# The feed-forward part of a decoder block in panels of Strassen products, its output added up in memory

## The reference, cut to what matters

```python
h = h + merged @ w_out[l]
hn = rms_norm(h, norm_ffn_g[l])
h = h + (jax.nn.silu(hn @ w_ffn_gate[l]) * (hn @ w_ffn_up[l])) @ w_ffn_down[l]
```

## Time and profile before

| | us |
|---|---|
| median of 3 runs (1349.11 to 1349.36) | 1349.15 |
| span of the profiled execution | 1347.3 |
| PE busy, share of the span | 1331.1, 99% |
| DVE busy, share | 743.3, 55% |
| ACT busy, share | 606.4, 45% |
| POOL busy | 33.5, 2% |
| moved by DMA | 251.23 MB, 186 GB/s over the span |

### The profile page before, as it was taken

One profiled execution on the slowest core, in us unless ns is written; L12 is line 12 of the kernel. 1 busy time (PEld: TensorE's weight loads), 2 busy tenths in 40 slices (PEclk: granted clock), 3 DMA queues, 4 the chain that ended last, 5 costly groups with the idle time before them and its releaser, 6 DMA issues.

```text
span 1347.3 us, 16021 instructions
## 1 busy us (share of the span) xinstructions
PE 1331.1 (99%) x6224; PEld 1100.3 (82%) x6224; DVE 743.3 (55%) x938; ACT 606.4 (45%) x781; POOL 33.5 (2%) x34
## 2 busy tenths in 40 slices
PE   7999999999999999999999999999999999999998
PEld 6888887777788888888888888888888888888887
DVE  6556556777455555565555555455545554555553
ACT  5454545555444444444444443344444434444442
POOL 1112110000000000000000000000000000000000
PEclk9999999999999999999999999999999999999999
DMA  8655655444565555555565555555555556555552
GB/s 260 198 202 165 210 188 182 147 148 143 206 200 188 188 187 188 188 185 187 188 193 185 191 188 201 194 188 188 189 186 188 187 200 196 195 187 187 187 187 94
DMA packets 129943, 251.23 MB, mean 186 GB/s; under 512 B 4624, under 2 KB 10832, under 8 KB 129632
## 3 DMA queue, kind: packets, MB, share of 16 engines
q1 hardware_dynamic: 129600, 250.37, 56.5%
q0 software_dynamic: 288, 0.10, 0.1%
HBM read 248.33 MB, written 2.12 MB: 186 GB/s over the span
## 4 chain that ended last, share of the span: by engine, by line
PE 95%; ACT 3%; DVE 1%; issue 0%; DMA 0%; DVEq 0%; SPq 0%; ACTq 0%
PE bank L948 30%; PE bank L950 30%; PE bank L949 30%; PE bank L877 2%; ACT prob L594 1%; PE bank L892 1%; ACT w_hi L494 1%; PE bank L917 1%; DVE staged L657 0%; PE bank L919 0%; PE bank L902 0%; DMA x_rows<-in_x 0%; PE bank L918 0%; DVE xT_lo L665 0%; DVE w_lo L648 0%
## 5 line engine op out<-in xcount | busy, mean ns | idle before, releaser
L648 DVE TENSOR_TENSOR w_lo<-raw,w_hi 128x1024 fp32r<-128x1024 f32 (+1 forms) x464 | 562.5, 1216 | 556.1 <-ACT w_hi L494 554.2
L494 ACT ACTIVATE w_hi<-raw 128x1024 fp32r<-128x1024 f32 (+1 forms) x464 | 487.6, 1052 | 694.8 <-PE bank L950 693.2
L948 PE MATMUL bank<-w_hi,xT_hi 128*128 128x512 f32 (+1 forms) x1248 | 488.6, 391 | 4.2 <-DVE w_lo L648 3.0
L950 PE MATMUL bank<-w_lo,xT_hi 128*128 128x512 f32 (+1 forms) x1248 | 483.2, 387 | 0.0
L949 PE MATMUL bank<-w_hi,xT_lo 128*128 128x512 f32 (+1 forms) x1248 | 482.9, 387 | 0.0
L948 PEld LDWEIGHTS bank<-w_hi,xT_hi 128*128 128x128 f32 x1248 | 234.9, 188 | 53.7 <-issue 2.6
L950 PEld LDWEIGHTS bank<-w_lo,xT_hi 128*128 128x128 f32 x1248 | 234.9, 188 | 47.9
L949 PEld LDWEIGHTS bank<-w_hi,xT_lo 128*128 128x128 f32 x1248 | 235.1, 188 | 45.8
L948 PE MATMUL bank<-w_hi,oT_hi 128*128 128x512 f32 x480 | 187.0, 390 | 0.0
L950 PE MATMUL bank<-w_lo,oT_hi 128*128 128x512 f32 x480 | 186.8, 389 | 0.0
L949 PE MATMUL bank<-w_hi,oT_lo 128*128 128x512 f32 x480 | 186.7, 389 | 0.0
(11 more groups left out here) (109 smaller groups left out, 496.2 us busy)
## 6 DMA issues: line engine op xcount, KB each, us to landing
raw<-in_w_in SPq DMA_DIRECT2D x64, 1024.0 KB, 5.3
raw<-in_w_ffn_gate SPq DMA_DIRECT2D x44, 1024.0 KB, 5.2
raw<-in_w_ffn_up SPq DMA_DIRECT2D x44, 1024.0 KB, 5.1
raw<-in_w_ffn_down SPq DMA_DIRECT2D x44, 1024.0 KB, 5.0
raw<-in_w_out SPq DMA_DIRECT2D x16, 1024.0 KB, 5.0
raw<-in_w_branch_a SPq DMA_DIRECT2D x8, 1024.0 KB, 5.0
raw<-in_w_branch_b SPq DMA_DIRECT2D x8, 1024.0 KB, 4.9
x_rows<-in_x SPq DMA_DIRECT2D x4, 512.0 KB, 7.7
```

Source lines behind the costliest of these rows:

```text
L494: A(w_hi[:, p % SPLIT_SLOTS, 0:w], raw[:, c % RAW_SLOTS, (p % 2) * w:(p % 2 + 1) * w], ACT.Copy).then_inc(hi_ready, 1)
L648: V.tensor_tensor(w_lo[:, p % SPLIT_SLOTS, 0:w], raw[:, p // 2 % RAW_SLOTS, (p % 2) * w:(p % 2 + 1) * w], w_hi[:, p % SPLIT_SLOTS, 0:w].bi ...
L948: M(sums, x_hi, w_hi[:, p % SPLIT_SLOTS, w], start=kt == 0, stop=False)
L950: ins = M(sums, x_hi, w_lo[:, p % SPLIT_SLOTS, w], start=False, stop=kt == j.kts - 1)
```

## The change

The FFN leaves the list of jobs and gets 17 panels. A panel of kind `gu` takes one column of 512 of gate and the same of up, a panel `down` two output columns; so a panel has two weight columns and two token tiles. Its first eight k-tiles are seen as a 2 x 2 matrix of blocks: left operand [token tile][k half], weight [k half][column], a k half being four k-tiles. Instead of eight block products there are Strassen's seven (in the form with running sums, M1 to M7). The k-tiles behind the first eight are units N0 to N3 of four k-tiles, for both token tiles, as before. N0 and N1 are of the first column, N2 and N3 of the second.

- **Units.** One split is of four k-tiles at once (128 x 2048): 11 for 16 k-tiles, 9 for 12. There are three slots (`UNIT_SLOTS`). M units have 12 matmuls, N units 24.
- **Weight sums in place.** With the raw blocks 11, 12, 21, 22 in SBUF: P = 11 + 12, R = P + 22, Z = 21 + R are made by DVE in the place of 11, 11 and 21; Q = 12 + 22 is made by an adding transfer from SBUF to SBUF that POOL issues (`sum_q`, 1 MB).
- **Loads.** Five slots (`QUAD_SLOTS`) of 1 MB and a planned order (`plan_loads`): a slot is reused when the low part of its last unit is made.
- **PSUM chained.** M1 is copied by ACT to a second bank and M6 added there by PE; DVE subtracts that from a copy of M5 to seed the two banks of the second column (`seed_c`, `seed_e`); M7, M3, M4 and the N units accumulate on top. The panel's N2 and N3 run inside the next panel.
- **Left sums.** Four combinations of the left blocks (`xs`, `fs`) are made by DVE once for all gu panels and once per block for `down`, and split.
- **Output.** `h` is stored to the output by POOL during the last `out` jobs; each `down` panel is copied to SBUF by ACT and added to the output in memory by two adding transfers of 0.5 MB (`add_out`).
- Panels are written out, without hardware loops. The split slots and raw slots of the FFN lie over those of the jobs.

The order of units and the loads:

```diff
+    index = first_index
+    for p in panels:
+        for name in ("M1", "N2-", "M5", "N3-", "M6", "M2", "M7", "N0", "M3", "N1", "M4"):
+            owner = p.prev if name[-1] == "-" else p
+            if owner is not None and name[0:2] in owner.unit:
+                p.order.append(owner.unit[name[0:2]])
+        if p is panels[-1]:
+            p.order += [p.unit[name] for name in ("N2", "N3") if name in p.unit]
...
+    needs = {"M1": ("11",), "M5": ("12",), "M6": ("22",), "M2": ("21",)}
...
+        slot = min(range(QUAD_SLOTS), key=lambda i: -1 if held[i] is None else last_use(held[i]))
+        load.slot = slot
+        if held[slot] is not None:
+            load.freed = ("sum", held[slot].panel) if held[slot].name == "11" else ("lo", last_use(held[slot]))
```

POOL:

```diff
+            out_view = out[0].rearrange("(t p) d -> p t d", p=P)
+            for n in range(NB):
+                cs = slice(n * COLS, (n + 1) * COLS)
+                pool.wait_ge(h_ready, n + 1)
+                pool.dma_start(out_view[:, :, cs], h[:, :, cs]).then_inc(h_stored, 16)
+            def sum_q(panel):
+                pool.wait_ge(quad_landed[panel.slot["22"]], panel.landed["22"])
+                pool.wait_ge(sum_ready, sums(panel, "P"))
+                pool.dma_start(quad[:, panel.slot["12"], :], quad[:, panel.slot["22"], :],
+                               accum_op=ALU.add).then_inc(q_summed, 16)
+            def add_out(panel, half):
...
+                pool.wait_ge(evacuated, T * (panel.down + 1))
+                pool.dma_start(out_view[:, :, cs], evac[:, half], accum_op=ALU.add).then_inc(added, 16)
```

ACT, the splits and the order:

```diff
+            def unit_hi(u):
+                panel, slot = u.panel, u.panel.slot[u.raw]
+                if u.name in ("M5", "M6", "M4"):
+                    act.wait_ge(sum_ready, sums(panel, {"M5": "P", "M6": "R", "M4": "Z"}[u.name]))
+                elif u.name == "M7":
+                    act.wait_ge(q_summed, 16 * (panel.n + 1))
+                else:
+                    act.wait_ge(quad_landed[slot], panel.landed[u.raw])
+                act.wait_ge(piece_used, u.index - UNIT_SLOTS + 1)
+                A(u_hi[:, u.slot, :], quad[:, slot, :], ACT.Copy).then_inc(hi_ready, 1)
...
+                    if u.name == "M6":
+                        copy_m1(panel)
+                    if u.name == "M7":
+                        copy_m5(panel)
+                    unit_hi(u)
+                    if panel.n == 0:
+                        if u.name == "M6":
+                            act.wait_ge(h_ready, NB)
...
+                        if u.name == "M2":
+                            scaled_to_hi(2 * NB - 1, NB - 1)
...
+                        if u.name == "M2":
+                            evacuate(before, 1, 0)
+                            evacuate(before, 1, 1)
```

DVE, the order:

```diff
+                for u in panel.order:
+                    if panel.n == 0 and u.name == "M5":
+                        sum_p(panel)
+                    if u.name == "M6" and panel.n == 0:
+                        sum_r(panel)
+                    if u.name == "M2" and panel.n == 0:
+                        add_to_h(jobs[-1], h_ready)
+                    unit_lo(u)
+                    if u.name == "M5" and panel.n:
+                        sum_r(panel)
+                    if u.name == "M2":
+                        sum_z(panel)
...
+                        elif before.kind == "gu":
+                            hidden(before)
+                    if u.name == "M7":
+                        seed_c(panel)
...
+                    if u.name == "M3":
+                        seed_e(panel)
+                        if before is not None and before.kind == "gu":
+                            hidden_lo(before)
+                    if u.name == "M4" and before is not None and before.kind == "gu" and before.block_slot == 1:
+                        forms_lo(before)
+                    if u.name == "M1" and before is not None and before.kind == "gu":
+                        sum_p(panel)
+                        gated(before, 0)
```

PE:

```diff
+                if u.name == "M7":
+                    pe.wait_ge(c_seeded, panel.n + 1)
+                    ins = product(u, b_bank(panel), *combined(panel, 2), False)
...
+                if u.name in ("N0", "N1", "N2", "N3"):
+                    left_ready(panel, u.kt0 // GROUP)
+                    top, bottom = (a_bank, b_bank) if u.name in ("N0", "N1") else (c_bank, e_bank)
+                    product(u, top(panel), *own(panel, u.kt0, 0), False)
+                    pe.wait_ge(e_seeded, panel.n + 1)
+                    ins = product(u, bottom(panel), *own(panel, u.kt0, 1), False)
```

More of the change, by code:

```diff
@@ L37 @@
 FF_BLOCKS = 4
+UNIT_KT = 4
+UNIT = UNIT_KT * COLS
+UNIT_SLOTS = 3
+QUAD_SLOTS = 5
 EPS = 1e-6
@@ L114, in plan @@
         job("out", n, "w_out", 0, n * COLS, COLS, kt, "m", 0)
[L115 to L126, removed]
     last_of, piece, sets = {}, 0, 0
@@ L143, in plan, with __init__, index, a_done @@
     return jobs, segments
+class Unit:
+    def __init__(self, panel, name, raw, kt0):
+        self.panel, self.name, self.raw, self.kt0 = panel, name, raw, kt0
+        self.index = self.slot = 0
+class Panel:
+    def __init__(self, n, kind, col, kts, prev):
+        self.n, self.kind, self.col, self.kts, self.prev = n, kind, col, kts, prev
+        self.block = self.block_slot = self.row = self.down = 0
+        self.unit, self.order = {}, []
+        self.slot, self.landed = {}, {}
+        for name, raw in (("M1", "11"), ("M5", "11"), ("M6", "11"), ("M2", "21"), ("M7", "12"), ("M3", "22"),
+                          ("M4", "21")):
+            self.unit[name] = Unit(self, name, raw, 0)
+        rest = kts // UNIT_KT - 2
+        for half in range(2):
+            for i in range(rest):
+                name = f"N{2 * half + i}"
+                self.unit[name] = Unit(self, name, name, (2 + i) * UNIT_KT)
+    def index(self, *names):
+        return max(self.unit[name].index for name in names if name in self.unit)
+    @property
+    def a_done(self):
+        return self.index("M2", "N0", "N1")
+    @property
+    def b_done(self):
+        return self.index("M4", "N0", "N1")
+    @property
+    def c_done(self):
+        return self.index("M3", "N2", "N3")
@@ new lines, with __init__, plan_panels, panel @@
+class Load:
+    def __init__(self, panel, name, half, kt0):
+        self.panel, self.name, self.half, self.kt0 = panel, name, half, kt0
+        self.slot, self.freed = 0, None
+def plan_panels(kt, ff_cols, d_cols, first_index):
+    panels = []
+    def panel(kind, col, kts):
+        panels.append(Panel(len(panels), kind, col, kts, panels[-1] if panels else None))
+        return panels[-1]
+    down = 0
+    for block, ff in enumerate(range(0, ff_cols, FF_BLOCKS)):
+        k = min(FF_BLOCKS, ff_cols - ff)
+        for i in range(k):
+            p = panel("gu", ff + i, kt)
+            p.block, p.block_slot = block, i
+        for m in range(d_cols // 2):
+            p = panel("down", m, k * GROUP)
+            p.block, p.row, p.down = block, ff * GROUP, down
+            down += 1
+    index = first_index
[6 more added lines that the diff above has]
+            p.order += [p.unit[name] for name in ("N2", "N3") if name in p.unit]
+        for u in p.order:
+            u.index = index
+            u.slot = (index - first_index) % UNIT_SLOTS
+            index += 1
+    return panels
@@ L161, in build @@
     assert T == 2 and KVA == P and QA == QB and HA == t5_bias.shape[1] and S == 4 * HD
-    jobs, segments = plan(D, QA, KVA, QB, w_ffn_gate.shape[2])
+    jobs, segments = plan(D, QA, KVA, QB)
+    PIECES = jobs[-1].piece0 + jobs[-1].pieces
+    panels = plan_panels(KT, w_ffn_gate.shape[2] // COLS, NB, PIECES)
+    units = [u for panel in panels for u in panel.order]
+    units.sort(key=lambda u: u.index)
+    loads = plan_loads(panels, units)
+    SETS = 1 + max(j.set for j in jobs if j.set is not None)
     weights = {"w_in": w_in, "w_branch_a": w_branch_a, "w_branch_b": w_branch_b, "w_out": w_out,
@@ L165, in build @@
     ATT_PIECE0 = next(j.piece0 for j in jobs if j.kind == "ga")
-    LAST_DOWN = jobs[-1].done
+    FIRST_OUT = next(j.piece0 for j in jobs if j.kind == "out")
     with ExitStack() as ctx:
@@ L574, in follow @@
                     scaled_to_hi(NB + j.n, j.n)
[L575 to L584, removed]
+                if j.kind == "out" and k == 6 and j.n == 0:
+                    A(x21[:], staged[:, 1, :], ACT.Copy).then_inc(x21_ready, 1)
+                if j.kind == "out" and k == 7 and j.n == 1:
+                    act.wait_ge(xs_summed, 1)
+                    A(xs_hi[:], xs[:], ACT.Copy).then_inc(xs_hi_ready, 1)
             def exp_scores(i):
@@ new lines, in evacuate, with copy_m5 @@
+            def evacuate(panel, half, t):
+                if t == 0 and panel.down:
+                    act.wait_ge((out_added0, out_added1)[half], 16 * panel.down)
```

(20 more changed lines are left out.)

368 lines of the change are left out of this document (316 added, 52 removed).

## The result

The changed kernel takes 1355.78 us (median of 4 runs, 1353.77 to 1357.54) against 1349.13: 1.0049 times the time of before (95% interval 1.0037 to 1.0061), slower by 6.6 us. I had forecast 1344.6.

The account below looks back on a forecast made before the run. PE, busy for 99% of the span, bounds the kernel. FFN 682.7 + 34.6 of gaps + 3 for the clock = 720.3 against 729.0 us (-8.7), end +4.2: -4.5, giving 1344.6 us, range 1337 to 1381.

Parts of the forecast that it names:

- Matmuls and durations: FFN: 204 fewer matmuls at 0.2268 us save 46.3 us; 2048-wide operations take DVE 2.31 us, ACT copies 1.95.
- Panel 0: First FFN panel: no earlier unit covers its serial sums; gaps of 19.4 us on PE, with Q late at M7.
- Left sums, copies, last block: Later panels: gaps of 3.1 us for left sums, 5.2 for ACT's copies after down panels, 6.3 in the last block.
- The transfers: Each panel: Q (6.0 us) and the load of 21 share engines evenly; load needs 8.2 of 8.6 us, hidden.
- Q goes first: Rival: Q takes most of the engines, load of 21 late in 16 panels, 37 us, 1365 to 1381; chance 0.26.
- The clock: Gap at M7 of panel 0: PE's clock falls toward its lower level, costing 3 us.
- The end: After the last matmul: two ACT copies and POOL's adding transfer take 8.9 us against 4.7 before; cost 4.2.
- two cases of a costly Q: Q taking the engines ahead of the load (0.26), or Q needing 10 us of them, about 1400 us (0.13).
- Q hidden: The forecast's own case: Q's transfer costs no time in the panels; range 1337 to 1351 us, chance 0.52.

Follow-up runs that it names:

- version at 1327 us: Changed kernel with Q issued behind the load of 21, panel 0 reordered, and the last output added by DVE and stored by SP: 1327.45 us (0.9846).

## Why the prediction was wrong, by its own steps

**Matmuls and durations: right.** 204 matmuls fewer; a gu panel without other trouble takes 41.73 us (41.7 said). DVE's 2048-wide operation took 2.29 us (2.31 said), its sums 2.28, ACT's copy 1.92 (1.95). Written-out code cost nothing.

**Panel 0: right in its steps, a little high in sum.** 19.2 us beyond the matmuls, 22.4 said (19.4 of gaps and 3 of clock). Counted from the start of M1, M5 started after 5.6 us (5.7 said), M6 after 12.1 (12.3), M2 after 18.8 (19.2), M7 after 28.6 (29.2 without Q, 30.5 with it). The 1.3 us for Q weren't paid: Q landed 21.9 us after M1's start, where 25.5 was said, and ACT's copy for M7 started at 23.7, behind the copy to `xT_hi` and that of M5.

**Left sums, copies, last block: nearly right.** Seen without Q: panels 2, 8 and 14 have 1.1 us too many (1.05 said), panels 5, 6, 11 and 12 1.3 to 1.4 (1.3 said). In the last block the gap ahead of N0 is 2.8 us (2.8 said), and the larger gaps of panel 16 are 0.8 and 1.7, where 0.9, 0.7 and 1.9 were said.

**The transfers: this step failed, in how the engines are shared.** Q's size was good: 5.6 us of the engines (6.0 taken), landing after 8.3 us (10.6 said for Q alone). But I let Q and the load of 21 share evenly from the load's issue on, 8.2 us for the load where 8.6 were to be had. In the fifteen panels in which the two meet it took 9.2 to 13.0 us, in the ten of the chain 9.9 to 13.0: in most of them the load started late, and it came out behind nearly all of Q, as in the rival *Q goes first*. The 12.4 to 13.0 us are panels 5, 11 and 12, where an adding transfer to the output is in flight too, which I had called free; with Q gone the load takes 7.8 to 9.3 us beside it, and ACT waits at most 1.2 us for it. Leaving Q out gives back 13.2 us, moving it 11.7. These two kernels measure 1342.6 and 1344.1, the forecast without this cost was 1344.6; that it comes so near is in part luck, since panel 0 took 3.2 us less than its term.

**The rival was priced too high.** I gave it 37 us with a Q of 6.0: each microsecond that the load is late was to cost one in 16 panels. It cost 11.7 in all. By a landing of 10.8 against 8.6 it should still be 2.2 x 16 = 35. Three things were left out.

- A slack behind ACT. In panel 7 ACT was free for the load 8.0 us after its issue and would have waited 0.8 more for PE, as it does there with Q behind the load; so the load was due after 8.8 and came after 10.3. PE lost 0.8 of these 1.5 us. By the prediction's own durations DVE has some 1.3 us in hand there: an idle time ahead of M2's low part, and a seed that is ready before M7 is due.
- Five panels with little or no cost. In panels 1, 2, 4, 10 and 14 the load took 9.2 to 9.9 us, and PE lost 0.5 us at most. In panel 16 the load is issued 12 us ahead of Q.
- Gaps that were there anyway. In panels 5, 6, 11 and 12 M7 comes 1.2 to 1.3 us late for ACT's copies, Q or not, and the late load lies beside that. In panel 6 it adds nothing.

**The clock: the mechanism was right, the places were not.** 3 us were said, for the gap ahead of M7 in panel 0. These windows of the changed kernel start at the gap of 2.9 us ahead of M5:

```profile
616.00:618.00 2.00, 0.86 (x4) 0.38 (x2) 0.78 (x1) 1.67 (x2) 0.00 (x0) 1.00 0.00 0
618.00:620.00 2.00, 0.43 (x1) 0.43 (x2) 2.00 (x2) 0.00 (x0) 0.00 (x0) 0.85 0.00 0
620.00:622.00 2.00, 2.00 (x6) 1.52 (x6) 1.71 (x1) 0.25 (x1) 0.00 (x0) 0.50 0.00 0
```

The granted clock is at its lower level, 1.2 of 2.4 GHz, already then. In the trace 40 matmuls show the longer duration of 0.63 us; they start 0.43 us apart (1.28 for three) where the others take 0.227, so 40 x 0.2 = 8 us of longer matmuls. Not all of it is a cost. 24 of them are in panel 0: the 15 in M5 and M6 ended before PE's next unit was ready, so they only shortened a gap (with Q behind the load M5 ran at full pace, and M6 started at the same 12.1 us). The 9 in M7 cost 1.8 us, less than the 3 said. The other 16 are in two `down` panels, from 858 and from 1295 us on, behind gaps of 2.2 and 3.4 us; they cost 3.2 us that had no term. The version at 1327 us has 7 such matmuls.

**The end: right.** 9.4 us from the last matmul (8.9 said, 4.7 before).

**Chances.** "Slower" had 0.42, nearly all of it on two cases of a costly Q. The forecast was put on Q hidden because its margin, 8.2 against 8.6, was positive. With no row of two queues at work, a margin of 0.4 us on an assumed even share wasn't worth more than the opposite.

## What to carry to other kernels

When a new transfer starts beside a load whose landing an engine waits for, count the load as coming behind the whole of it, and let whichever has the longer slack be issued later: one wait on POOL was worth 11.7 us here. Before such a lateness is multiplied by the number of panels, follow it to the bounding engine: here about a third of what was reckoned arrived. When work is taken from the bounding engine, look at the first unit of the new scheme and at the end: no neighbour covers them, and more than half of the 28.3 us between the changed kernel and the best version lay there. A copy moved from one engine's queue to another moves the gap with it, if both queues stand ahead of the same unit or the next.

## What the runs showed of the hardware that I had not expected

An adding transfer of 1 MB inside SBUF takes the 16 engines 5.6 us, 1.8 times the 3.1 us of a load of the same size, and lands 8.3 us after its issue; cut to rows of 2 KB it lands after 10.8 beside a load. A load issued 1.5 us behind it moved its first packet 4.5 us after its issue, not 1.2; where both queues were at work, they moved as many packets the one as the other (115 and 120, 108 and 106), whatever their length. An adding transfer of 0.5 MB to memory at the end takes 7.8 us from issue to the end of the span, a store 3.3.

The granted clock doesn't follow from the length of a gap alone. A gap of 2.9 us ahead of M5 was enough in the changed kernel for it to fall to 0.50; the same gap with Q behind the load left M5 at full pace, and in the version at 1327 us a gap of 2.3 us left M6 at full pace and one of 2.2 us didn't leave M1 so. Behind a gap of 2.2 us it fell in panel 5 (0.59 from 858 to 860 us) and not in panels 11 and 12; gaps of about 1 us left the matmuls behind them at full pace in the changed kernel.
